# The experts' gate and up products computed by features: weight blocks stationary, 128 token columns moving, slot weights applied to the output rows

## What is computed

```
for e in range(N_EXPERTS):                       # 16 experts, top-2 of them for each token
    he = silu(t @ w1[e]) * (t @ w3[e])           # w1, w3: 1024 x 512 each
    y = y + combine[:, e:e + 1] * (he @ w2[e])   # w2: 512 x 1024; combine: the token's weight for e
x = x + gate2 * y
```

## Time and profile before

| what | us |
|---|---|
| three runs | 1320.29, 1319.44, 1321.06 (median 1320.29) |
| the profiled execution | 1321.44 |
| its span, first to last instruction | 1319.7 |
| PE busy | 1260.3 (96%) |
| PEld, DVE, ACT, POOL busy | 726.8, 561.8, 233.8, 284.7 |
| mean granted TensorE clock, share of full speed | 0.992 |

### The profile page before, as it was taken

How to read it: one execution, slowest core, us unless ns; L and a number is a source line. 1 busy time by engine, 2 the same in 40 slices (tenths; PEclk the granted TensorE clock), 3 DMA queues, 4 the chain that set the end, 5 groups by cost and what they waited for, 6 DMA issues and landing times.

```text
span 1319.7 us, 11735 instructions
## 1 busy us (share of the span) xinstructions
PE 1260.3 (96%) x4533; PEld 726.8 (55%) x4534; DVE 561.8 (43%) x999; ACT 233.8 (18%) x485; POOL 284.7 (22%) x205
## 2 busy tenths in 40 slices
PE   3999998999999999999999999999899999999995
PEld 1444466444576767767777777545444444444442
DVE  2322257344186783584245336365522222222222
ACT  3211256113272002001100110111110101010100
POOL 0124000444003233232223331000103131313121
PEclk9999999999999999999999999999899999999998
DMA  9742320013000111111222135411799888888750
GB/s 344 279 171 88 132 72 1 16 64 136 8 1 0 64 64 65 64 64 64 71 102 83 64 145 222 144 48 64 278 424 382 318 360 327 358 321 358 307 226 33
DMA packets 59284, 209.00 MB, mean 158 GB/s; under 512 B 8992, under 2 KB 9312, under 8 KB 53088
## 3 DMA queue, kind: packets, MB, share of 16 engines
q1 hardware_dynamic: 46480, 185.72, 36.6%
q0 software_dynamic: 12000, 20.48, 4.4%
q10 hardware_dynamic: 752, 2.11, 0.4%
HBM read 208.24 MB, written 23.10 MB: 175 GB/s over the span
## 4 chain that ended last, share of the span: by engine, by line
PE 87%; DVE 6%; issue 2%; SPq 2%; ACT 1%; DMA 1%; POOL 0%; POOLq 0%; DVEq 0%; ACTq 0%
PE psum L1596 30%; PE psum L1754 17%; PE psum L1482 10%; PE psum L1773 8%; PE psum L1544 5%; PE psum L1660 4%; PE psum L1533 3%; PE psum L1578 3%; PE psum L1434 2%; SPq L429 1%; DMA weight_ring<-in_w_ada 1%; DVE arena L1082 1%; PE psum L1733 1%; PE psum L1560 1%; DVE softmax_stats L1051 1%
## 5 line engine op out<-in xcount | busy, mean ns | idle before, releaser
L1596 PE MATMUL psum<-arena,weight_ring 128*128 128x320 f32 x928 | 256.9, 432 | 0.0
L1754 PE MATMUL psum<-weight_ring,arena 128*128 128x512 f32 x512 | 222.7, 592 | 0.7 <-ACT arena L840 0.7
L1596 PEld LDWEIGHTS psum<-arena,weight_ring 128*128 128x128 f32 x928 | 175.9, 190 | 72.7
L1596 PE MATMUL psum<-x,weight_ring 128*128 128x320 f32 x640 | 180.0, 433 | 2.1 <-DVE arena L1106 2.1
L1754 PEld LDWEIGHTS psum<-weight_ring,arena 128*128 128x128 f32 x512 | 96.1, 190 | 115.2 <-issue 114.3
L1596 PEld LDWEIGHTS psum<-x,weight_ring 128*128 128x128 f32 x640 | 120.9, 190 | 52.4 <-DVE arena L1106 3.1
L1482 PE MATMUL psum<-weight_ring,arena 128*128 128x512 f32 x320 | 140.6, 593 | 2.1 <-DVE arena L924 1.6
L1773 PE MATMUL psum<-arena 128*128 128x512 f32 x256 | 112.6, 593 | 0.7 <-ACT arena L848 0.7
L584 POOL TENSOR_TENSOR weight_ring<-weight_ring 128x1024 f32<-128x1024 f32 x14 | 35.0, 2497 | 347.9 <-DMA weight_ring<-in_w_in 151.6
L1482 PEld LDWEIGHTS psum<-weight_ring,arena 128*128 128x128 f32 x320 | 59.4, 190 | 71.2 <-issue 68.7
L1106 DVE TENSOR_TENSOR arena<-psum,arena 128x320 f32<-128x320 f32 x124 | 59.4, 487 | 84.9 <-PE psum L1596 84.3
(11 more groups left out here) (253 smaller groups left out, 1328.1 us busy)
## 6 DMA issues: line engine op xcount, KB each, us to landing
weight_ring<-in_w SPq DMA_DIRECT2D x32, 2048.0 KB, 12.0
weight_ring<-in_w_in SPq DMA_DIRECT2D x16, 2048.0 KB, 7.7
arena<-in_w SPq DMA_DIRECT2D x16, 2048.0 KB, 10.6
weight_ring<-in_w_ada SPq DMA_DIRECT2D x8, 2048.0 KB, 10.6
weight_ring<-in_w_ada SPq DMA_DIRECT2D x8, 1024.0 KB, 14.6
x<-in_x_sample SPq DMA_DIRECT2D x2, 2048.0 KB, 13.4
weight_ring<-in_w_conv_out SPq DMA_DIRECT2D x2, 2048.0 KB, 7.8
weight_ring<-in_w_attn_out SPq DMA_DIRECT2D x2, 2048.0 KB, 8.0
```

What stands on the lines that cost most here:

```text
L1596: last = mm(product_psum(q, name), w[:, k, :], src[:, k, :], start=(k == 0), stop=(k == 3))
L1754: last = mm(psum[:, 1024 + 512 * j:1536 + 512 * j], xgT[:, t, :], w[:, t, :], start=(t == 0), stop=(t == KT - 1))
```

## The change

The gate and up products change sides. A block of weights, 128 features by 128 hidden features, is stationary, and `xgT`, 128 features by 128 slots, moves. The result comes out by hidden features, 4 blocks of 128 (loop over `f`), each with the 128 slots as columns. This is the layout that the down product wants. So `hidden_T` goes on PE, its copy on ACT, and `hh`; DVE writes the product of silu and up straight into `hhT`, which gets two buffers. The slot's weight, which lies by slot, can't multiply these rows by features with a per-partition scalar. It moves into the product with the gate row in `add_rows`. The semaphore for gate and up is split, so that ACT can start the silu when the gate half is done, and PE waits at the start of the up half for the last reader of the up bank. w2 is loaded with its rows in another order, `(k p) n` for `(p k) n`.

```diff
-        hh = at(Z + 512, 512)
-        hhT = at(Z + 1024, 512).rearrange("p (k s) -> p k s", k=4)
+        hhT = [at(Z + 512 + 512 * b, 512) for b in range(2)]
...
         def down_src(e):
-            return io["w2"][e].rearrange("(p k) n -> p k n", p=P)
+            return io["w2"][e].rearrange("(k p) n -> p k n", p=P)
...
-            def gate(k):
-                act.wait_ge(s_gu, k + 1)
+            def gate(k, first=False):
+                act.wait_ge(s_gate_done, k + 1)
+                if not first:
+                    act.wait_ge(s_hh, k)
                 A(sg, psum[:, 1024:1536], ACT.Silu).then_inc(s_sg, 1)
-
-            def hidden_T(k):
-                act.wait_ge(s_HT, k + 1)
-                A(hhT.rearrange("p k s -> p (k s)"), psum[:, 2048:2560], ACT.Copy).then_inc(s_hhT, 1)
...
-            def hidden(k, weight):
+            def hidden(k, b):
                 dve.wait_ge(s_sg, k + 1)
-                V.scalar_tensor_tensor(out=hh, in0=psum[:, 1536:2048], scalar=weight, in1=sg,
-                                       op0=mult, op1=mult).then_inc(s_hh, 1)
+                dve.wait_ge(s_gu, k + 1)
+                V.tensor_tensor(hhT[b], psum[:, 1536:2048], sg, mult).then_inc(s_hh, 1)
...
-                    V.tensor_tensor(part, psum[:, 2560 + 512 * half:3072 + 512 * half], part, mult).then_inc(s_prod, 1)
+                    V.scalar_tensor_tensor(out=part, in0=psum[:, 2560 + 512 * half:3072 + 512 * half], scalar=weight, in1=part,
+                                           op0=mult, op1=mult).then_inc(s_prod, 1)
...
+                    if j == 1 and not first:
+                        pe.wait_ge(s_hh, k)
                     w = gu_slot[2 * b + j].rearrange("p (k n) -> p k n", k=KT)
-                    for t in range(KT):
-                        last = mm(psum[:, 1024 + 512 * j:1536 + 512 * j], xgT[:, t, :], w[:, t, :], start=(t == 0), stop=(t == KT - 1))
-                last.then_inc(s_gu, 1)
-
-            def hidden_T(k):
+                    for f in range(4):
+                        out = psum[:, 1024 + 512 * j + P * f:1152 + 512 * j + P * f]
+                        for t in range(KT):
+                            last = mm(out, w[:, t, P * f:P * (f + 1)], xgT[:, t, :], start=(t == 0), stop=(t == KT - 1))
+                    last.then_inc((s_gate_done, s_gu)[j], 1)
+
+            def down_proj(k, loaded, value, b, hidden_b, first=False):
                 pe.wait_ge(s_hh, k + 1)
-                for t in range(4):
-                    every = hh.rearrange("p (q k) -> p k q", k=4)
-                    last = tr(psum[:, 2048 + P * t:2048 + P * (t + 1)], every[:, t, :], ident[:, :])
-                last.then_inc(s_HT, 1)
...
                     gate_up(e, s_wgu[b], it * 64 + 32 * ((3 + j) // 2 + 1), b)
                     tokens_T(e + 1, s_xg[j], it * 16 + 32, j)
-                    down_proj(e - 1, s_wd[1 - b], it * 32 + 16 * ((2 + j) // 2 + 1), 1 - b)
-                    hidden_T(e)
+                    down_proj(e - 1, s_wd[1 - b], it * 32 + 16 * ((2 + j) // 2 + 1), 1 - b, 1 - b)
```

More of the change, by code:

```diff
@@ L362, in build @@
         s_xg = [sem(f"tokens_gathered{b}") for b in range(XG)]
-        s_T, s_xgT, s_gu, s_sg, s_hh, s_HT, s_hhT, s_d = (sem(n) for n in (
-            "xg_transposed", "xgT_copied", "gate_up_done", "silu_done", "hidden_ready", "hidden_transposed", "hiddenT_copied", "down_done"))
+        s_T, s_xgT, s_gate_done, s_gu, s_sg, s_hh, s_d = (sem(n) for n in (
+            "xg_transposed", "xgT_copied", "gate_done", "gate_up_done", "silu_done", "hidden_ready", "down_done"))
         s_gate, s_prod = sem("slot_gates_ready"), sem("y_gated")
@@ L860, in _ @@
                               .to_broadcast([P, D])).then_inc(s_g2rows, 16)
-            gate(0)
+            gate(0, first=True)
             tokens_T(1)
-            hidden_T(0)
             with act.Fori(1, EXPERTS - 1) as e:
@@ L867, in _ @@
                 tokens_T(e + 1)
-                hidden_T(e)
             gate(EXPERTS - 1)
-            hidden_T(EXPERTS - 1)
             def more(e, c, k):
@@ L874, in more @@
                 gate(k + EXPERTS)
-                hidden_T(k + EXPERTS)
             more_chunks(act, more)
@@ L1377, in slot_gates, with add_rows @@
                                        op1=add).then_inc(s_gate, 1)
-            def add_rows(k, b, landed=None):
+            def add_rows(k, b, weight, landed=None):
                 dve.wait_ge(s_gate, k + 1)
@@ L1391, in add_rows, with chosen @@
                 V.tensor_tensor(acc_ctx[b], acc_ctx[b], gated, add).then_inc(s_y, 1)
+            def chosen(e):
+                return slice(ORDER[e] * CHUNKS, ORDER[e] * CHUNKS + 1)
             for e in range(EXPERTS):
-                chosen = slice(ORDER[e] * CHUNKS, ORDER[e] * CHUNKS + 1)
-                hidden(e, w_slot[:, chosen])
+                hidden(e, e % 2)
                 if e == 1:
                     gate_difference()
-                    slot_gates(is_ctx[:, ORDER[0] * CHUNKS:ORDER[0] * CHUNKS + 1])
+                    slot_gates(is_ctx[:, chosen(0)])
                 if e:
-                    add_rows(e - 1, (e - 1) % 2, 32 * e)
+                    add_rows(e - 1, (e - 1) % 2, w_slot[:, chosen(e - 1)], 32 * e)
                     dve.wait_ge(s_y, e)
-                    slot_gates(is_ctx[:, chosen])
-            add_rows(EXPERTS - 1, (EXPERTS - 1) % 2, 32 * EXPERTS)
+                    slot_gates(is_ctx[:, chosen(e)])
+            add_rows(EXPERTS - 1, (EXPERTS - 1) % 2, w_slot[:, chosen(EXPERTS - 1)], 32 * EXPERTS)
             def more(e, c, k):
-                hidden(k + EXPERTS, w_now)
+                hidden(k + EXPERTS, 0)
                 dve.wait_ge(s_y, k + EXPERTS)
                 slot_gates(ctx_now[:, 0:1])
-                add_rows(k + EXPERTS, 0)
+                add_rows(k + EXPERTS, 0, w_now)
             more_chunks(dve, more)
@@ L1751, in gate_up @@
                         weight_table()
+                    if j == 1 and not first:
+                        pe.wait_ge(s_hh, k)
                     w = gu_slot[2 * b + j].rearrange("p (k n) -> p k n", k=KT)
-                    for t in range(KT):
-                        last = mm(psum[:, 1024 + 512 * j:1536 + 512 * j], xgT[:, t, :], w[:, t, :], start=(t == 0), stop=(t == KT - 1))
-                last.then_inc(s_gu, 1)
-            def hidden_T(k):
-                pe.wait_ge(s_hh, k + 1)
-                for t in range(4):
-                    every = hh.rearrange("p (q k) -> p k q", k=4)
-                    last = tr(psum[:, 2048 + P * t:2048 + P * (t + 1)], every[:, t, :], ident[:, :])
-                last.then_inc(s_HT, 1)
-            def down_proj(k, loaded, value, b, first=False):
-                pe.wait_ge(s_hhT, k + 1)
+                    for f in range(4):
[4 more added lines that the diff above has]
+            def down_proj(k, loaded, value, b, hidden_b, first=False):
+                pe.wait_ge(s_hh, k + 1)
                 if not first:
@@ L1772, in down_proj @@
                     for t in range(4):
-                        last = mm(psum[:, 2560 + 512 * half:3072 + 512 * half], hhT[:, t, :], w[:, t, 512 * half:512 * (half + 1)],
-                                  start=(t == 0), stop=(t == 3))
+                        last = mm(psum[:, 2560 + 512 * half:3072 + 512 * half], hhT[hidden_b][:, P * t:P * (t + 1)],
+                                  w[:, t, 512 * half:512 * (half + 1)], start=(t == 0), stop=(t == 3))
                     last.then_inc(s_d, 1)
@@ L1783, in _ @@
             tokens_T(1, s_xg[1], 16, 1)
-            hidden_T(0)
             gate_up(1, s_wgu[1], 32, 1)
             tokens_T(2, s_xg[2], 16, 2)
-            down_proj(0, s_wd[0], 16, 0, first=True)
-            hidden_T(1)
+            down_proj(0, s_wd[0], 16, 0, 0, first=True)
             gate_up(2, s_wgu[0], 64, 0)
             tokens_T(3, s_xg[3], 16, 3)
-            down_proj(1, s_wd[1], 16, 1)
-            hidden_T(2)
+            down_proj(1, s_wd[1], 16, 1, 1)
             with pe.Fori(0, 3) as it:
@@ L1798, in _ @@
                     tokens_T(e + 1, s_xg[j], it * 16 + 32, j)
-                    down_proj(e - 1, s_wd[1 - b], it * 32 + 16 * ((2 + j) // 2 + 1), 1 - b)
-                    hidden_T(e)
+                    down_proj(e - 1, s_wd[1 - b], it * 32 + 16 * ((2 + j) // 2 + 1), 1 - b, 1 - b)
             gate_up(15, s_wgu[1], 32 * 8, 1)
-            down_proj(14, s_wd[0], 16 * 8, 0)
-            hidden_T(15)
-            down_proj(15, s_wd[1], 16 * 8, 1)
+            down_proj(14, s_wd[0], 16 * 8, 0, 0)
+            down_proj(15, s_wd[1], 16 * 8, 1, 1)
             def more(e, c, k):
@@ L1808, in more @@
                 gate_up(k + EXPERTS, s_ofw, (k + 1) * 48, 0)
-                hidden_T(k + EXPERTS)
-                down_proj(k + EXPERTS, None, 0, 0)
+                down_proj(k + EXPERTS, None, 0, 0, 0)
             more_chunks(pe, more)
```

## The result

The changed kernel takes 1323.53 us (median of 13 runs, 1321.24 to 1324.48) against 1319.88 (13 runs, 1319.27 to 1321.06). The ratio is 1.0022, with a 95% interval of 1.0013 to 1.0030: slower by 1.7 to 4.0 us. The profiled execution took 1323.83 us, its span 1322.1.

What follows compares the result with a forecast made beforehand. The prediction took TensorE's unbroken instruction stream to bound the experts' stage. Its terms, +9.0 - 6.6 - 0.2 + 0.1 = +2.3 us, gave 1323.7 on the profiled execution and 1322.6 us on the median's scale, range 1317.5 to 1335.

Steps and rivals of the forecast that it cites:

- Gate and up: Experts' gate and up products: 128 passes at 0.1117 us, 14.30 us instead of 13.74, 16 times on the path, +9.0 us.
- hidden_T: Hidden transposes leave TensorE: 0.47 us saved for each of experts 1 to 14, none for 0 and 15, -6.6 us.
- The wait behind expert 0's gate half: Before expert 0's up half: the gate half ending 0.28 us later swallows TensorE's 0.2 us wait for VectorE, -0.2 us.
- VectorE: Two gate-row products on the chain at the end grow from 692 to 751 ns, +0.1 us.
- At nothing: Experts' stage: removed ScalarE copy, earlier silu, new TensorE and ScalarE waits and w2's 4 KB rows cost nothing.
- faster distance: Rival on gate and up: passes settle at 0.110 us, total 1319.0 us, or 1313.6 at the 0.1073 floor; chance 0.15.
- loads in line: Rival on gate and up: each pass loads, then streams, 0.232 us, about 1569 us in all; chance under 0.01.
- Loads slowed: Rival on gate and up: weight loads slow passes to 0.1175 us amid DMA traffic, sum +14, 1334.5 us; chance 0.09.
- Code and issue: Rival in the experts' loop: record supply or code fetches leave TensorE holes, 1368 or 1335 us, mostly +3 to +15; chance 0.18.

Runs made afterwards that it cites:

- e1: Kernel before with only the gate and up products cut into four 128-column pieces, hidden transposes kept: 1328.83 us against 1320.22, ratio 1.0070.
- e5: Changed kernel with 96 of the 128 token columns moving in the gate and up products, one execution: 1322.08 us.
- e6: Changed kernel with 96 of the 128 weight columns of each block held still, one execution: 1316.65 us.
- e2: Changed kernel with gate and up back to 16 products of 512 columns, hidden transposes still left out: 1314.48 us, ratio 0.9952 to the kernel before.
- e9: Changed kernel with output rows gathered earlier and the last down product waiting half by half for VectorE: 1319.49 us, ratio 0.9994 to the kernel before.
- e4: Kernel before with only the slot weights moved from the hidden product to the two gate-row products: 1320.20 us against 1320.22, ratio 1.0000.
- e3: Changed kernel with w2 loaded in the old row order, (p k) n: 1323.28 us, ratio 1.0024 to the kernel before.
- e7: Changed kernel with blocks of every fourth weight column held still and w2 in the old order, one execution: 1571.87 us against 1321.35.

## Why the prediction was right

The forecast was 1322.6 us, 0.17% more; it measured 1323.53, 0.22% by the ratio and 0.28% by the two medians, inside the range of 1317.5 to 1335. It had put 0.45 on no change and 0.43 on slower, with the border at 0.2%. The kernel is slower than before, for the interval of 0.13 to 0.30% leaves zero out, but it holds that border, so the runs don't decide between the two. By its own steps:

1. Gate and up, +9.0 us. A pass was taken at 0.1117 from the attention's value product. It takes 0.1116, and 16 x (14.29 - 13.74) = +8.8; e1, which has this term alone, shows +8.7 in the stage. The choice among four rows of 0.110 to 0.1175 was what made the forecast, and the criterion was shape and kind: two passes, 128 columns held, 128 moving. e5 and e6 show why it was right to ask for both: the load sets this pace, and the rows at 0.110 hadn't such a load in such a product. Why the number lies above 0.1073 the prediction had not right, for it said that 32-bit passes stream slowly enough to cover a load. With 128 moving columns they fall short of that by the 2.5 ns between e6 and the changed kernel.

2. hidden_T, -6.6 us. The stage gives -6.2 (e2) to -6.5 (e1 to changed). For expert 0 I counted nothing and it gave 0.2: 2.15 us from the token transposes to the next products, for 2.33. For expert 15 I counted nothing on the chain, rightly. But I said down(15) would be ready 1.2 us earlier, and it is 0.3 (from the start of down(14) to the end of down(15) 15.0 us for 15.3). I hadn't looked at what else down(15) waits for: VectorE's product on down(14) was late next. It cost nothing because the chain passes elsewhere; in e9, where it passes there, the same wait had to be split first.

3. The wait behind expert 0's gate half, -0.2 us: wrong. I let a longer product swallow a wait for VectorE. The up half starts 10.4 us after the gate half's first product (949.65 to 960.05), and it was 10.1 before (949.46 to 959.58): all of the 0.28 us came through. TensorE still waits twice for 0.2 us among the sums, and VectorE waits there for TensorE (7.5 us in two waits and 0.8 in one, by the same list), so VectorE's work moved with TensorE's. A wait on an engine that waits for you isn't slack.

4. VectorE, +0.1 us: the changed products at the end last 0.76 for 0.70 us. e4 shows nothing more than that.

5. At nothing: the new waits, the earlier silu, w2's rows. No TensorE wait belongs to them, and e3 shows w2's order at nothing. The one new wait with a price of its own is down(15)'s of 0.9 us, which lies off the chain.

My terms make +2.3 us, and the stage shows +2.2. That they meet to 0.1 us is in part luck: the 0.2 us of step 3 didn't come and the 0.2 us of expert 0's transposes, which I hadn't counted, did. The changed profile's span shows +2.4, the medians +3.65 with 1.7 to 4.0. The last 1.3 us are inside what the medians leave open. e3, the same kernel but for w2, has medians 3.1 us above before at a stage of +2.4. The 13 runs of the changed kernel fall into two groups, six from 1321.24 to 1322.43 and seven from 1323.53 to 1324.48, and those of before spread over 1.8 us. The profiled execution is in the upper group, and it is the one that lost 1.7 us to the lower clock at 490 us. That would fit the distance of the groups, but the other runs have no profile, so what the medians add to the +2.2 isn't shown, nor why the changed kernel's runs would meet it more often.

The rivals: the faster distance is refuted by the rows above, as is "loads in line". "Loads slowed" by traffic is too: at a DMA share of 0.77 to 0.88 in the loop's three rounds the stage runs at attention's pace. What I set against it doesn't carry over, though. I blamed the spread-out source for the 0.1175 of the transposes, a small thing, and e7 shows that in these products such a source more than doubles a pass. "Code and issue" is refuted for this size: 256 records go through in 14.29 us, one each 56 ns, 16 times over, where the densest long stretch before had 67; and five packets of code are kept.

The rule of the Trainium skill ("TensorE: Matmul & The Clock Gate", section "Back-to-back issue gap"), by which I had estimated 2.5 times for narrow products, doesn't hold for these 32-bit passes; it is 1.04. What that section of the Trainium skill says besides, that weight load and product both set the spacing, the traces bear out: the pass stays at 0.1114 us when a quarter of the moving columns goes (e5) and falls to 0.1091 when a quarter of the held ones does (e6).

## What to carry to other kernels

When a product is cut into narrower ones, take its pace from a row with the same number of held and moving columns and the same kind of product, and multiply out. Here 4 ns a pass decided (0.1116 for 0.1073), and four times the passes cost 4%. Before choosing a layout that saves transposes, look at the strides it puts on the operands: in narrow passes two elements apart cost 5% on the held side, and four apart took twice the time on either side. And when a stage leaves a list, ask what the next instruction waits for besides it.

## What the runs showed of the hardware that I hadn't expected

- A 32-bit pass with its held or its moving operand's columns four elements apart takes 0.232 or 0.227 us instead of 0.1116; with two elements, 0.1177 (held). A transpose holds its source as well and isn't slowed like this: 0.1175 with four elements, 0.110 with eight.
- Loads of 128 contiguous columns follow each other every 0.1116 us beside products, and loads of 96 every 0.1091, while their records last 192 and 163 ns: the record is longer than the pace.
- TensorE takes 256 records in 14.29 us, one each 56 ns, for 16 stretches, with DMA engines busy 0.77 to 0.88 of the time in the loop.
- A loop of 4 x 304 records of products and loads ran three rounds. Five packets of 16 KB, which I take for its code, were brought in the first round and none in the others.
